# Latent attention's scores over 128 channels as three products of high and low halves, with the value tiles copied by ScalarE

## The reference, cut to what matters

```python
def mla_core(q, k, v):
    s = jnp.einsum('bqhd,bkhd->bhqk', q, k).astype(F32) * ((C_NOPE + C_ROPE) ** -0.5)
    p = jax.nn.softmax(s, axis=-1)
    return jnp.einsum('bhqk,bkhd->bqhd', p.astype(v.dtype), v)
...
q = (rms_norm(cq, q_norm_w) @ wq_b).reshape(bsz, length, C_HEADS, C_NOPE + C_ROPE)
...
kv = (rms_norm(ckv, kv_norm_w) @ wkv_b).reshape(bsz, length, C_HEADS, C_NOPE + C_V)
k_rope_h = jnp.broadcast_to(k_rope[:, :, None, :], (bsz, length, C_HEADS, C_ROPE))
return jnp.concatenate([kv[..., :C_NOPE], k_rope_h], axis=-1), kv[..., C_NOPE:]
```

## Time and profile before

| | |
|---|---|
| median of 3 runs | 1072.35 us (1072.02 to 1072.69) |
| profiled execution | 1071.89 us |
| its span, first to last instruction | 1069.9 us |
| TensorE busy | 1049.8 us (98%) |
| VectorE busy | 733.3 us (69%) |
| ScalarE busy | 591.8 us (55%) |
| mean granted TensorE clock | 0.997 |
| data moved | 165.41 MB, mean 155 GB/s |

### The profile page before, as it was taken

How to read it: one execution, slowest core, us unless ns; L and a number is a source line. 1 busy time by engine, 2 the same in 40 slices (tenths; PEclk the granted TensorE clock), 3 DMA queues, 4 the chain that set the end, 5 groups by cost and what they waited for, 6 DMA issues and landing times.

```text
span 1069.9 us, 18034 instructions
## 1 busy us (share of the span) xinstructions
PE 1049.8 (98%) x6797; PEld 884.3 (83%) x6797; DVE 733.3 (69%) x1577; ACT 591.8 (55%) x1209; POOL 2.6 (0%) x10
## 2 busy tenths in 40 slices
PE   5999999999999999999999999999999999999997
PEld 3677776788997779989898988889988898888886
DVE  4635567665588756787778766658788778765665
ACT  4534245543364446568776764445567677665444
POOL 0000000000000000000000000000000000000000
PEclk9999999999999999999999999999999999999999
DMA  9998551222342224564555566666464545555662
GB/s 326 336 311 245 181 184 41 60 60 75 83 135 55 78 78 126 140 175 138 138 141 155 145 170 182 193 196 177 129 171 139 139 139 157 157 162 177 194 213 83
DMA packets 203551, 165.41 MB, mean 155 GB/s; under 512 B 7101, under 2 KB 172713, under 8 KB 203465
## 3 DMA queue, kind: packets, MB, share of 16 engines
q1 hardware_dynamic: 202944, 163.28, 52.0%
q0 software_dynamic: 192, 0.66, 0.2%
q10 hardware_dynamic: 328, 0.32, 0.1%
HBM read 163.18 MB, written 1.05 MB: 153 GB/s over the span
## 4 chain that ended last, share of the span: by engine, by line
PE 89%; DVE 7%; ACT 2%; issue 1%; DMA 1%; SPq 0%; ACTq 0%; DVEq 0%
PE pj L2059 23%; PE pj L2061 22%; PE pj L2060 22%; DVE w_lo L1328 2%; PE pj L2153 2%; PE tr L2611 1%; PE ac L2415 1%; PE ac L2550 1%; PE sc L2259 1%; PE tr L2266 1%; PE sc L2401 1%; ACT w_hi L835 1%; PE ac L2280 1%; PE sc L2532 1%; PE sc L2530 1%
## 5 line engine op out<-in xcount | busy, mean ns | idle before, releaser
L1328 DVE TENSOR_TENSOR w_lo<-raw,w_hi 128x1024 fp32r<-128x1024 f32 (+2 forms) x258 | 309.4, 1202 | 148.7 <-ACT w_hi L835 147.8
L835 ACT ACTIVATE w_hi<-raw 128x1024 fp32r<-128x1024 f32 (+2 forms) x258 | 268.0, 1040 | 89.3 <-PE pj L2061 87.3
L2059 PE MATMUL pj<-h_hi,w_hi 128*128 128x256 f32 (+1 forms) x960 | 299.0, 311 | 0.2
L2061 PE MATMUL pj<-h_hi,w_lo 128*128 128x256 f32 (+1 forms) x960 | 291.1, 303 | 0.0
L2060 PE MATMUL pj<-h_lo,w_hi 128*128 128x256 f32 (+1 forms) x960 | 291.0, 303 | 0.0
L2059 PEld LDWEIGHTS pj<-h_hi,w_hi 128*128 128x128 f32 x960 | 183.7, 191 | 19.1 <-issue 10.4
L2061 PEld LDWEIGHTS pj<-h_hi,w_lo 128*128 128x128 f32 x960 | 183.8, 191 | 7.4
L2060 PEld LDWEIGHTS pj<-h_lo,w_hi 128*128 128x128 f32 x960 | 184.0, 192 | 6.2
L2059 PE MATMUL pj<-w_hi,h_hi 128*128 128x512 f32 x344 | 137.4, 399 | 0.4 <-DVE h_lo L1402 0.4
L2061 PE MATMUL pj<-w_hi,h_lo 128*128 128x512 f32 x344 | 134.2, 390 | 0.0
L2060 PE MATMUL pj<-w_lo,h_hi 128*128 128x512 f32 x344 | 134.2, 390 | 0.0
(11 more groups left out here) (358 smaller groups left out, 1473.4 us busy)
## 6 DMA issues: line engine op xcount, KB each, us to landing
raw<-in_w_in_dram SPq DMA_DIRECT2D x152, 512.0 KB, 3.7
ada_raw<-in_ada_w_dram SPq DMA_DIRECT2D x48, 512.0 KB, 7.9
raw<-in_even_w_in_dram SPq DMA_DIRECT2D x28, 512.0 KB, 5.0
raw<-in_w_branch_dram SPq DMA_DIRECT2D x24, 512.0 KB, 3.7
raw<-in_w_out_dram SPq DMA_DIRECT2D x16, 512.0 KB, 3.7
raw<-in_odd_w_in_dram SPq DMA_DIRECT2D x11, 512.0 KB, 3.9
raw<-in_even_w_out_dram SPq DMA_DIRECT2D x8, 512.0 KB, 3.7
raw<-in_odd_w_out_dram SPq DMA_DIRECT2D x8, 512.0 KB, 3.8
```

The lines of the kernel that those rows point to most:

```text
L835: last = nc.scalar.activation(hi, src, ACT.Copy)
L1328: last = nc.vector.tensor_tensor(lo, src, hi.bitcast(F32), ALU.subtract)
L2059: nc.tensor.matmul(dst, lh, rh, start=first, stop=False)
L2061: return nc.tensor.matmul(dst, ll, rh, start=False, stop=final)
```

## The change

The 128-channel part of the scores is computed as all projections are: three products of halves instead of one float32 matmul. ScalarE writes the high half of queries and keys (`qn_hi`, `kn_hi`) and counts `nope_hi`; VectorE waits for it, subtracts (`qn_lo`, `kn_lo`) and frees the bank. The low halves lie in parts of `m_hi`, `m_lo`, `h_hi` and `h_lo` that are not in use then; a key's low half is in two pieces of 256 columns. All eight value tiles are copied by ScalarE instead of VectorE, and `keys_evacuate` goes. At the start, TensorE's `spread(0, 4)` moves behind `condition(1)`, `condition_turn(1)` ahead of `turn_x(4)`, and ScalarE's `ada_evacuate(2)` ahead of `modulated_hi(0, 1)`. At the end, the mean square is scaled by a quarter, and the reciprocal with its Newton step becomes reciprocal, multiply and add, reciprocal.

```diff
@@ chunk_groups
     if name == "wkv":
-        keys = [("kn", 4 * i + j, "dve" if 4 * i + j in DVE_KEYS else "act") for j in range(4)]
-        return keys + [("vm", (i, t), "dve") for t in range(4)]
+        return [("kn", 4 * i + j, "dve") for j in range(4)] + [("vm", (i, t), "act") for t in range(4)]
     if name == "wq":
-        return [("qn", 2 * i, "act"), ("qn", 2 * i + 1, "act"), ("qr", i, "act")]
+        return [("qn", 2 * i, "dve"), ("qn", 2 * i + 1, "dve"), ("qr", i, "act")]
...
+NOPE_ORDER = [(k, i) for k, i, _, _ in G1 if k in ("qn", "kn")]
...
-        qn_o = work[:, 512:2560].rearrange("p (h n) -> p h n", h=C_HEADS)
+        qn_hi = parts_o[:, 512:2560].rearrange("p (h n) -> p h n", h=C_HEADS)
+        qn_lo = [w[:, 3072 + SEQ * h:3072 + SEQ * h + SEQ] for w in (m_hi, m_lo) for h in range(C_HEADS // 2)]
...
-        kn_o = work[:, 3584:7680].rearrange("p (h n) -> p h n", h=C_HEADS)
+        kn_hi = parts_o[:, 3584:7680].rearrange("p (h n) -> p h n", h=C_HEADS)
+        kn_lo = [w[:, 2 * h:2 * h + 2, CTX] for w in (h_hi, h_lo) for h in range(C_HEADS // 2)]
@@ ScalarE, start
             x_turned_to(6)
+            ada_evacuate(2)
             modulated_hi(0, 1)
             x_turned_to(7)
             for pair in range(1, 4):
-                ada_evacuate(2 * pair)
+                if pair > 1:
+                    ada_evacuate(2 * pair)
                 ada_evacuate(2 * pair + 1)
@@ ScalarE, l1_evacuate
-                    if kind == "vm" or (kind == "kn" and engine == "dve"):
-                        continue
...
                     elif kind == "kn":
-                        nc.scalar.activation(kn_o[:, i, :], src, ACT.Copy).then_inc(freed["act"], 1)
+                        nc.scalar.activation(kn_hi[:, i, :], src, ACT.Copy).then_inc(nope_hi, 1)
+                    elif kind == "vm":
+                        half, n = i
+                        nc.scalar.activation(v_o[:, n, 512 * half:512 * half + 512], src, ACT.Copy).then_inc(freed["act"], 1)
                     elif kind == "qn":
-                        nc.scalar.activation(qn_o[:, i, :], src[:, 0:SEQ], ACT.Copy, scale=MLA_SCALE).then_inc(freed["act"], 1)
+                        nc.scalar.activation(qn_hi[:, i, :], src[:, 0:SEQ], ACT.Copy, scale=MLA_SCALE).then_inc(nope_hi, 1)
@@ VectorE, l1_evacuate
-                    elif kind == "vm":
-                        half, n = i
-                        proj_ready(dve, g, None)
-                        nc.vector.tensor_scalar(v_o[:, n, 512 * half:512 * half + 512], bank(g), 1.0, None, ALU.mult)\
+                    elif kind == "qn":
+                        dve.wait_ge(nope_hi, NOPE_ORDER.index((kind, i)) + 1)
+                        nc.vector.scalar_tensor_tensor(qn_lo[i], bank(g)[:, 0:SEQ], MLA_SCALE, qn_hi[:, i, :].bitcast(F32),
+                                                       ALU.mult, ALU.subtract).then_inc(freed["dve"], 1)
+                    elif kind == "kn":
+                        dve.wait_ge(nope_hi, NOPE_ORDER.index((kind, i)) + 1)
+                        nc.vector.tensor_tensor(kn_lo[i], bank(g).rearrange("p (a n) -> p a n", a=2),
+                                                kn_hi[:, i, :].bitcast(F32).rearrange("p (a n) -> p a n", a=2), ALU.subtract)\
                             .then_inc(freed["dve"], 1)
...
-                if s == WKV_SLOT[1]:
-                    for i in DVE_KEYS:
-                        keys_evacuate(i)
@@ VectorE, end (last_gained scales its part by the same quarter)
-                nc.vector.scalar_tensor_tensor(v, y_squares[:, 2 + n:3 + n], 1.0 / D, col[:, 1, 2 + n:3 + n], ALU.mult, ALU.add)\
+                nc.vector.scalar_tensor_tensor(v, y_squares[:, 2 + n:3 + n], 0.25 / D, col[:, 1, 2 + n:3 + n], ALU.mult, ALU.add)\
                     .then_inc(last_mean, 1)
                 dve.wait_ge(last_root, n + 1)
-                after(nc.vector.reciprocal(y, root))
-                newton(y, term, v).then_inc(last_set, 1)
+                after(nc.vector.reciprocal(term, root))
+                after(nc.vector.scalar_tensor_tensor(term, term, v, root, ALU.mult, ALU.add))
+                nc.vector.reciprocal(y, term).then_inc(last_set, 1)
@@ TensorE, start
             condition(0)
             turn_x(3)
-            spread(0, 4)
             condition_turn(0)
             condition(1)
+            spread(0, 4)
+            condition_turn(1)
             turn_x(4)
-            condition_turn(1)
             turn_x(5)
@@ TensorE, l1_scores
                 for e in range(2):
-                    nc.tensor.matmul(sc[:, e, :], qn_o[:, 2 * hp + e, q], kn_o[:, 2 * hp + e, :], start=True, stop=False)
+                    h = 2 * hp + e
+                    nc.tensor.matmul(sc[:, e, :], qn_hi[:, h, q], kn_hi[:, h, :], start=True, stop=False)
+                    nc.tensor.matmul(sc[:, e, :], qn_lo[h][:, q], kn_hi[:, h, :], start=False, stop=False)
+                    nc.tensor.matmul(sc[:, e, :].rearrange("p (a n) -> p a n", a=2), qn_hi[:, h, q], kn_lo[h], start=False,
+                                     stop=False)
```

More of the change, by code:

```diff
@@ L155, in chunk_groups @@
     return [(name, i, last[name])]
-DVE_KEYS = (4, 5)
 VALUE_NAMES = ("av", "bv")
@@ L432, in build_program @@
         w_hi, w_lo = sb("w_hi", [P, NSPLIT, WEL], F32R), sb("w_lo", [P, NSPLIT, WEL], F32R)
+        with nc.sbuf_tensor("parts_o", [P, 7680], F32R) as parts_o:
+            pass
         work = sb("work", [P, 12288])
@@ L579, in build_program @@
         recip_set = sem("recip_set")
+        nope_hi = sem("nope_hi")
         og_set, g_hi_set, g_lo_set = sem("og_set"), sem("g_hi_set"), sem("g_lo_set")
@@ L2020, in last_gained @@
                 dve.wait_ge(y_sq, n + 1)
-                part = nc.vector.tensor_scalar(col[:, 1, 2 + n:3 + n], y_squares[:, n:n + 1], 1.0 / D, NORM_EPS, ALU.mult, ALU.add)
+                part = nc.vector.tensor_scalar(col[:, 1, 2 + n:3 + n], y_squares[:, n:n + 1], 0.25 / D, 0.25 * NORM_EPS, ALU.mult,
+                                               ALU.add)
                 after(part)
```

## The result

The changed kernel took 1079.82 us (median of 4 runs, 1077.73 to 1080.26), the kernel before beside it 1072.18 us (1071.45 to 1072.69): ratio 1.0073, 95% interval 1.0058 to 1.0088. It is slower, as forecast, but by more: the prediction had 1076.8 us as the likeliest time and 1079.2 us as its upper end.

What follows compares the result with a forecast made beforehand. TensorE was taken to set the pace, with VectorE nearly full. -2.72 + 6.88 - 0.7 - 0.2 = +3.26 us on 1072.35 gave 1075.6, plus 1.2 for the clock 1076.8 us; range 1072.3 to 1079.2 us.

Steps and rivals of the forecast that it cites:

- Part 1: Scores' 128-channel part: six fp32r products at 0.23 us replace 1.72 us, saving 0.34 us a step, 2.72 us in all.
- Part 2: Query and key banks freed later, by VectorE: TensorE stalls before key 0 and key 7, together 6.88 us.
- Part 3: New order at the kernel's start: fourth conditioning product 0.7 us earlier; bounds 0 and -0.9 us.
- my bound 0: Bound on the start's gain: nothing gained, as the weights' transfers become the limit.
- Part 4: End of the kernel: one small instruction less around the reciprocal, -0.2 us; bounds -0.1 and -0.25 us.
- Part 5: Granted clock falls behind the 3.8 us stall, adding 1.2 us; the 2.9 us stall may add 1.0 us.
- case C: Both stalls before the key groups, clock falling twice: 1077.8 us, or 1078.5 if type changes cost 0.7 us; chance 0.18.
- B: As rival: both stalls before the key groups, clock stays up: 1075.6 us; chance 0.20.
- D: Only the first stall real (3.8 us of waits), key 4's low half getting ahead: 1072.5 us; chance 0.11.
- E: No stall left before the key groups, low halves freeing the banks in time: 1068.7 us; chance 0.09.

Runs made afterwards that it cites:

- start_only: The kernel before with only the new order at the start: 1071.44 us against 1070.93, ratio 1.0006.
- after_again: The changed kernel run again unaltered: 1077.24 us, ratio 1.0062 to the kernel before.
- filled: The changed kernel with unread 512-column products in TensorE's two stalls, 12 ahead of key 0 and 15 ahead of key 7: 1074.97 us, ratio 1.0035 to before.

## Why the prediction was off, by its own steps

**Part 1, the scores: right.** Products 0.23 us apart, 0.34 us a step; the saving alone was run and is there. The Trainium skill, FP8 and Floating Point Precision, TensorE Precision Notes, counts four passes for true FP32. An estimate by that page, at one pass for each product, is 1.29 us for the six; the trace has 1.38.

**Part 2, the stalls: right in place, cause and size.** The first gap was forecast as 2.9 us of idleness and is 2.79; the second as 3.8 and is 3.59. In sums: A without a fall is 14.64 - 11.63 = 3.01 us longer, with 0.34 of savings in it, so 3.35 us where 3.50 was forecast; B is 2.61 us longer with 0.68 of savings, so 3.29 where 3.38 was. Together 6.64 for 6.88. The order VectorE works in is what I read: in the changed kernel's timeline,

```profile
335.66 1.02 DVE L1335 TENSOR_TENSOR w_lo<-raw,w_hi 128x512 fp32r<-128x512 f32 x2
336.60 0.75 DVE L1723 SCALAR_TENSOR_TENSOR m_hi<-pj,parts_o 128x256 fp32r<-128x256 f32 x2
...
358.14 1.02 DVE L1335 TENSOR_TENSOR w_lo<-raw,w_hi 128x512 fp32r<-128x512 f32 x2
359.08 1.88 DVE L1727 TENSOR_TENSOR h_lo<-pj,parts_o 128x512 fp32r<-128x512 f32 x3
```

the query's low half directly behind the weights' (336.60 - 0.67 of late start = 335.93 us, forecast 335.92), the key's behind the next weights'. ScalarE's value copies cost nothing, as said.

**Part 3, the start: right in its place, but luck in the first profile, and nothing of it in the sum.** The 0.77 us wait is gone, and the fourth conditioning product starts at 22.87 us where it started at 24.57. But 0.90 of these 1.70 us are there at the first one, ahead of every instruction of TensorE that the change moved:

```profile
12.26 1.07 PE L2158 MATMUL sc<-ada_raw,cond 128*32 128x256 f32 x16
...
22.87 1.07 PE L2158 MATMUL ac<-ada_raw,cond 128*32 128x256 f32 x16
```

and in the kernel before, with the head sums at 215 us:

```profile
13.16 1.75 PE L2153 MATMUL sc<-ada_raw,cond 128*32 128x256 f32 x16
...
215.50 1.95 PE L2290 MATMUL tr<-ones,scr 128*128 128x1 f32 x16
```

Taken from the first conditioning product, the fourth comes 11.53 us later in the mean of the seven traces with the old start and 10.73 us later in the ten with the new one: 0.80 us gained, for 0.7. At the head sums 0.6 us of it are left (202.39 and 201.79 us from the first conditioning product). In the first profile the wait of 0.7 us for conditioning weights, at 66.6 us, took the order's gain back (the case of my bound 0), and the inputs' early arrival put 0.90 us in its place, so the head sums start at 214.61 us, 0.89 us sooner. Then comes the fall near 217 us. From the first head sums to the second it is 19.36 to 19.39 us in the four traces with that fall and 17.81 or 17.82 in the nine with unsplit sums and none, so this fall costs 1.56 us, and -0.89 becomes the +0.67 of the table above. The times of `start_only` show no gain (1.0006 [0.9994, 1.0017]).

**Part 4, the end: right in kind, smaller than forecast.** From the first reciprocal to the scaling of the last half it is 0.66 us (1073.20 to 1073.86) where it was 0.78 (1065.28 to 1066.06): 0.12 us for 0.2. The fused step takes 0.22 us where the steps before took 0.16. It is too small to be told apart in the times.

**Part 5, the clock: this is the step that failed.** "I expect the clock to fall behind it ... I take 1.2 us": one fall of 3.4 us, its length from the earlier trace rows. A fall of that length cost 1.1 to 1.3 us behind the stalls, so the price was right. The lengths and the number of falls were not. Behind these stalls a fall mostly lasts 6.8 us and costs 2.0 to 2.4 us, and both stalls can bring one: in the five traces with both stalls open the cost was 3.3, 2.2, 2.3, 2.2 and 3.5 us, 2.7 us on average. Even case C, two falls, was priced at 2.2 us (1077.8 less 1075.6). The earlier trace rows could not show this: its fall comes in a stretch in which TensorE was busy 4.00 of 4.00 us, so it says that the clock can fall, and nothing of what an idle gap does; and I took the length of that one fall for a stronger disturbance. The Trainium skill, TensorE: Matmul & The Clock Gate, section What's actually happening, says of a kernel's start that the number of slow products varies from run to run. The traces show the same in the middle of a kernel (0, 3.4 and 6.8 us behind the same stall), and the forecast should have been a spread. Part 5 also had no term for a fall elsewhere, and the one near 217 us cost 1.56 us.

The arithmetic of the miss, for the first trace: the clock in A and B 3.3 us for 1.2 (+2.1), the fall near 217 us, for which there was no term (+1.6), the start up to the head sums -0.89 for -0.7 (-0.2), the end -0.1 for -0.2 (+0.1), the stalls 6.64 for 6.88 (-0.2). That is +3.4 us in the spans. The medians are 0.2 us closer to each other than the spans (7.64 us for 7.8), and the kernel before was 0.2 us faster beside the changed one than in the prediction: +3.0 us, and 1079.82 is 3.0 above 1076.8. Most of the miss is thus the clock's. How large it came out was in part chance: three of the four runs, the profiled one among them, had a mean clock of 0.990, while `after_again`, the same kernel, had 0.990 in one of four and by its ratio stands at 1.0062 x 1072.18 = 1078.8 us.

The rivals B (no fall), D and E (fewer stalls) are out: of the five traces with both stalls open none has both stretches at full clock, and both stalls are in every one. C, two falls, is nearest to the first trace. B's 1075.6 us is what `filled` measures, by its ratio 1.0035 x 1072.18 = 1075.9.

## What to carry to other kernels

When an operation that frees a buffer moves to another engine, go through that engine's program order between the buffer's last write and the free: here VectorE had only 1.9 us more to do by my sum, and the low halves' places behind a weight split and a softmax cost 6.6 us. Price a stall on TensorE at its length and add the clock as a spread: here stalls of 2.8 and 3.6 us cost 2.2 to 3.5 us more for it. Take the stall away by order before judging the change: the same edit went from 1.007 to 0.998. To split a loss into waiting and clock, fill the gap with unread products of the same length.

## What the runs showed of the hardware

- A gap of 2.79 us was followed by 6.8 us at 1.2 GHz in two of six traces in which it stood open, by 3.4 us in one, by none in three. A gap of 3.59 us was followed by 6.8 us in four of five and by 3.4 us in one. The falls that began inside the gap were the 6.8 us ones, those that began behind it the 3.4 us ones.
- The granted clock fell also without any idleness: near 217 us behind 1.95 us of one-column products, in a stretch in which TensorE was busy all the time, in some executions and not in others. It cost 1.56 us, more than the 1.1 to 1.3 us of a fall of the same length behind a stall. The first trace of the changed kernel:

```profile
214.61 1.95 PE L2295 MATMUL tr<-ones,scr 128*128 128x1 f32 x16
216.42 0.47 PE L2064 MATMUL pj<-h_hi,w_hi 128*128 128x512 f32 x1
216.74 0.44 PE L2065 MATMUL pj<-h_lo,w_hi 128*128 128x512 f32 x1
216.98 0.63 PE L2066 MATMUL pj<-h_hi,w_lo 128*128 128x512 f32 x1
```

- The times of the kernel before come in steps: 28 of 78 runs had a mean clock of 0.999 and a median span of 1067.3 us, 32 had 0.997 and 1069.6 us. The fall near 217 us is in none of the seven traces with the old start, so it is hardly the step. The one near 440 us stood in 12 of 17 traces; from the end of B to the end of the span it is 711.3 us with it and 709.9 without in kernels with the scores of before, 709.5 and 708.0 in the changed ones, so it costs 1.5 us. That it makes most of the step of 2.3 us is likely and not shown, as no trace of a run of the kernel before at 0.999 was kept.
